# One reciprocal for the softmax sums of two attention units

## What is computed

```python
# nsa_mixer: 16 heads; compressed, selected and windowed keys, each output gated
o = g[..., 0:1] * o_cmp + g[..., 1:2] * o_sel + g[..., 2:3] * o_win
# swa_sink_mixer: 16 heads, window of 128 keys, a sink logit per head
m = jnp.maximum(jnp.max(s, axis=-1, keepdims=True), sk)
e = jnp.exp(s - m)
p = e / (jnp.sum(e, axis=-1, keepdims=True) + jnp.exp(sk - m))
# neighbourhood_attention (8 heads, 512 keys, with a bias) and
# memory_cross_attention (4 heads, 256 keys): p = softmax(s)
```

## Time and profile before

| | |
|---|---|
| median of 3 runs | 2753.83 us (2752.65 to 2754.45) |
| the profiled execution | 2753.48 us, its span 2751.7 us |
| PE busy | 2563.0 us, 93% of the span |
| POOL busy | 1775.8 us, 65% |
| DVE busy | 1378.4 us, 50%, in 2631 instructions |
| ACT busy | 698.0 us, 25% |
| mean granted clock of TensorE | 0.962 |

### The profile page before, as it was taken

How to read it: one execution, slowest core, us unless ns; L and a number is a source line. 1 busy time by engine, 2 the same in 40 slices (tenths; PEclk the granted TensorE clock), 3 DMA queues, 4 the chain that set the end, 5 groups by cost and what they waited for, 6 DMA issues and landing times. The chain is left out here.

```text
span 2751.7 us, 36593 instructions
## 1 busy us (share of the span) xinstructions
PE 2563.0 (93%) x11854; PEld 2052.2 (75%) x11854; DVE 1378.4 (50%) x2631; ACT 698.0 (25%) x1475; POOL 1775.8 (65%) x983
## 2 busy tenths in 40 slices
PE   7798888899999888899999899999999899999998
PEld 6676666688888667688888587777777776787876
DVE  6378888433442477422112466666128534652552
ACT  3302777211001227211101222232006323100001
POOL 5364444577777567587777444445779867687784
PEclk9898999999999989999999999999999999999999
DMA  7573000254652220233333222212333223233332
GB/s 254 153 214 118 1 1 16 61 178 158 213 176 84 62 62 26 86 98 99 92 98 93 84 62 62 62 54 62 94 103 65 72 61 111 84 94 97 92 103 73
DMA packets 420546, 260.13 MB, mean 95 GB/s; under 512 B 62844, under 2 KB 411513, under 8 KB 414017
## 3 DMA queue, kind: packets, MB, share of 16 engines
q1 hardware_dynamic: 390811, 191.28, 24.2%
q10 hardware_dynamic: 29606, 67.22, 7.2%
HBM read 254.25 MB, written 8.10 MB: 95 GB/s over the span
## 5 line engine op out<-in xcount | busy, mean ns | idle before, releaser
L654 POOL TENSOR_TENSOR W<-RAW,zeros 128x1024 fp32r<-128x1024 f32 (+2 forms) x355 | 680.5, 1917 | 698.7 <-PE PA L735 335.2
L661 POOL TENSOR_TENSOR W<-RAW,W 128x1024 fp32r<-128x1024 f32 (+2 forms) x355 | 851.7, 2399 | 48.2 <-PE PA L741 22.0
L734 PE MATMUL PA<-H,W 128*128 128x512 f32 x1272 | 506.4, 398 | 6.4 <-DVEq L2289 2.3
L735 PE MATMUL PA<-H,W 128*128 128x512 f32 x1272 | 495.6, 390 | 0.0
L734 PE MATMUL PA<-A,W 128*128 128x512 f32 x944 | 381.1, 404 | 16.0 <-DVE A L1921 10.8
L735 PE MATMUL PA<-A,W 128*128 128x512 f32 x944 | 378.5, 401 | 0.0
L741 PE MATMUL PA<-H,W 128*128 128x512 f32 x1272 | 316.3, 390 | 0.0
L734 PEld LDWEIGHTS PA<-H,W 128*128 128x128 f32 x1272 | 238.9, 188 | 64.2 <-POOL W L654 6.9
L735 PEld LDWEIGHTS PA<-H,W 128*128 128x128 f32 x1272 | 238.8, 188 | 54.5 <-issue 5.5
L741 PEld LDWEIGHTS PA<-H,W 128*128 128x128 f32 x1272 | 238.9, 188 | 49.3
L741 PE MATMUL PA<-A,W 128*128 128x512 f32 x944 | 249.7, 402 | 0.0
(11 more groups left out here) (362 smaller groups left out, 3919.2 us busy)
## 6 DMA issues: line engine op xcount, KB each, us to landing
AD<-in_ada_w_dram ACTq DMA_DIRECT2D x40, 1024.0 KB, 5.5
RAW<-in_w_in_dram SPq DMA_DIRECT2D x160, 256.0 KB, 3.1
RAW<-in_mlp_w_up_dram SPq DMA_DIRECT2D x128, 256.0 KB, 3.1
RAW<-in_mlp_w_down_dram SPq DMA_DIRECT2D x128, 256.0 KB, 3.0
RAW<-in_w_up_dram SPq DMA_DIRECT2D x88, 256.0 KB, 3.1
RAW<-in_nsa_w_in_dram SPq DMA_DIRECT2D x40, 256.0 KB, 4.1
RAW<-in_w_down_dram SPq DMA_DIRECT2D x16, 384.0 KB, 3.4
RAW<-in_swa_w_in_dram SPq DMA_DIRECT2D x20, 256.0 KB, 3.3
```

Of the source, the lines that this page charges most:

```text
L654: e.tensor_tensor(W[0][:, s, 0:kc], RAW[:, s, 0:kc], zeros[:, 0:1].rearrange("p (a b) -> p a b", b=1).broadcast_to([P, kc, P]), ALU.add).t ...
L661: e.tensor_tensor(W[1][:, s, 0:kc], RAW[:, s, 0:kc], W[0][:, s, 0:kc].bitcast(F32), ALU.subtract).then_inc(w_split, 1)
L734: pe.matmul(PA[s][:, 0:n], W[0][:, s, k], hi, start=(k == 0), stop=False)
L735: mm = pe.matmul(PA[s][:, 0:n], W[0][:, s, k], lo, start=False, stop=False)
```

## The change

The plan gets a list `slot`: a column of the statistics for each unit, which counts single units only and starts anew in each plan. In a plan single units stand in even numbers between `all` units, so b0 and b1 always have columns 2k and 2k+1, and b2 and b3 the next two. On DVE the reciprocal of an even slot is left out; behind the mask that follows the odd one's, one instruction over two columns takes both, and raises `inverted` by 2. The wait for `exped` stands ahead of the branch and is kept in every step.

```diff
@@ class Plan, number
+            single = list(itertools.accumulate(int(not self.groups[G]["all"]) for G, _ in self.units))
+            self.slot = [(n - 1) % 8 for n in single]
@@ POOL, scale_weights
-                nk, v = grp["keys"][b], u % 8
+                nk, v = grp["keys"][b], plan.slot[i]
@@ ACT, attention
-                    nk, sink, v = grp["keys"][b], grp["sink"], u % 8
+                    nk, sink, v = grp["keys"][b], grp["sink"], plan.slot[i]
@@ DVE, attention
-                    nk, mask, v = grp["keys"][b], grp["mask"][b], u % 8
+                    nk, mask, v = grp["keys"][b], grp["mask"][b], plan.slot[i]
...
-                    else:
-                        dve.reciprocal(stat[3][:, u % 8:u % 8 + 1], stat[2][:, u % 8:u % 8 + 1]).then_inc(sem("inverted"), 1)
+                    elif plan.slot[i - 1] % 2:
+                        v = plan.slot[i - 1]
+                        dve.reciprocal(stat[3][:, v - 1:v + 1], stat[2][:, v - 1:v + 1]).then_inc(sem("inverted"), 2)
```

## The result

The kernel after takes **2759.8 us** (median of 20 runs, 2756.8 to 2771.2), the kernel before 2752.2 us in the runs beside it (20 runs, 2745.2 to 2754.5). The ratio is **1.0041** (95% interval 1.0031 to 1.0051): slower by 0.4%, some 11 us. The medians alone are 7.6 us apart; the runs of either kernel scatter over 9 us and more. The profiled execution took 2761.91 us, its span is 2759.8 us, and the mean granted clock is 0.961 where it was 0.962.

A forecast was written before the change was run, and what follows sets the result against it. Bounds: DVE and PE fullest in nsa, no single one in swa, POOL in na, DVE nearly empty in ca. Terms -1.0 - 0.1 + 1.1 + 0.2 = +0.2 us gave 2753.7, as a median 2754.0 us; range 2750.5 to 2758.0.

The forecast's parts named there:

- paid once, not eight times: In na, POOL's wait for the later pair costs +1.1 us (0 to +2.2) in total, not in every head.
- if DVE's times stay: Condition in na: with DVE's timing unmoved, POOL lags 1.1 us and later heads find the pair ready.
- in later heads the bias add then falls on L661 in front, which stretches: In na, POOL's L661 lengthens beside DVE's add by as much as the even unit's multiplication no longer does.
- Are DVE's times unmoved?: In na, yes: DVE's 1.28 us wait is for ACT, not POOL, and scores are ready before DVE asks.
- nsa, -1.0: In nsa, a fifth of the 5.1 us for 64 removed reciprocals is gained: -1.0 us, between 0 and -5.1.
- The cover is PE's distance of five units: In nsa, later multiplications on POOL cost 0, because PE runs five units behind.
- swa, -0.1: In swa, removed reciprocals gain the low end, -0.1 us of a possible 2.6; the delay costs 0.
- ca, +0.2: In ca, the last pair's later multiplication costs +0.2 us, between 0 and +1.2, mostly hidden behind other PE work.
- rival C: In swa, POOL comes too late for PE's transposes: 0.1 to 0.5 us in 16 heads, 2 to 8 us; chance 0.09.
- Rival A: In na, the delay is paid per head through late scores: 8 to 15 us, 2761 to 2769 us; chance 0.06.
- Rival B: In nsa and swa, every removed reciprocal counts at least 0.08 us: 2747.4 us, at the far end 2735; chance 0.05.
- Rival D: In nsa and swa, shifted steps move TensorE's granted clock: 2.5 us either way per stretch, 2751.5 to 2756.5 us; chance 0.12.

The follow-up runs named there:

- c1: Kernel after, but single reciprocals in na and for the two units ahead of nsa's `all` unit: ratio to the kernel before 1.0004 (0.9993 to 1.0015).
- d2: Kernel before, single reciprocals kept, with nsa's 128x4 product done twice in each head, the second waiting for the first: ratio 1.0014 (1.0004 to 1.0024).
- c2: c1 plus, in na, the next head's bias add taken two steps earlier: ratio to the kernel before 0.9995 (0.9984 to 1.0005).
- b1: As a run, not the unit: kernel after with na's value split moved behind the pair's reciprocal; one run, 2766.8 us.
- b2: As a run, not the unit: kernel after with na's next-head bias add moved two steps earlier; one run, 2762.2 us.
- b3: As a run, not the unit: kernel after with both na moves, late value split and early bias add; one run, 2752.0 us.

## Why the prediction was wrong

The forecast was 2754.0 us, the measurement 2759.8, above the range. By its own steps:

1. **na, "paid once, not eight times": the step that failed.** It forecast +1.1 us, and na lost 8.7. The first half held: in the head of the earlier trace rows POOL waits 2.2 us for the pair (2.15 forecast), and b2 and b3 together take 3.11 us, against 3.14 forecast. In the second head even the rest came as forecast: L663 (2082.34) took 3.19 us and POOL did not wait. What failed is "if DVE's times stay" with "in later heads the bias add then falls on L661 in front, which stretches". From the fourth head on L663 did not stretch (2.39 us), in the third hardly (2.52); DVE's split of the values did, from 0.43 to 2.00 us, and pushed the add behind L663. The stretch of 4.24 for 3.14 had been read as something that only POOL suffers. The earlier trace rows The contest has two sides, and the side that gives way decides: when POOL gives way, POOL's lag is absorbed, when DVE does, POOL's next wait is renewed. The question "Are DVE's times unmoved?" was answered from what DVE waits for, not from the durations of its instructions, and the 2.35 us of the add at 2083.57 went unread. The second half of that answer failed too: "the scores behind them are ready before DVE asks", but DVE's mask of b2 waits 0.84 us for them (2115.16). How na's 8.7 us divide between the held split and these late scores is not shown: no run takes away one and leaves all else.
2. **nsa, -1.0.** It was +4.0. That removed reciprocals are mostly swallowed was right (c1: 48 of 64 win nothing that can be told). "The cover is PE's distance of five units" left out the compressed unit, whose product and multiplication follow the late pair in the same step and which PE reaches with little slack: 0.2 us of delay (d2) is enough for 2.8 us more of waits. The 4.0 us itself is one execution's; 1.0 to 5.9 us were seen with the same order.
3. **swa, -0.1, and ca, +0.2.** Measured -0.6 and -0.2 in the profiled executions. Over all of the table swa takes 79.6 to 80.0 us with the pairs and 80.2 to 80.8 without, a gain of 0.2 to 1.2. The stage is shorter, not longer, so rival C's price did not occur.
4. **Rival A** had the right shape and price, 8 to 15 us for a delay in every head, and a chance of 0.06. Its chain is there up to a point: PE's transposes wait for POOL, 10.4 us in na where it was 1.7, and DVE then waits for scores, 12.3 us where it was 6.0. But it does so at the mask of b2, and not "in front of the bias add or the b0 mask", and A has no word of the held split. **Rival B** is excluded: with 88 pairs kept (48 in nsa, 32 in swa, 8 in ca) c1's ratio is 1.0004 (0.9993 to 1.0015), while 0.08 us for each would be 7 us, or 0.26%. **Rival D:** nsa's granted clock went from 0.91 to 0.90, and that is not the loss: in the same stretch (262 to 474 us) c2 has 0.88 and 213.7 us, b1 0.91 and 218.8. na's went from 0.98 (2063 to 2163 us) to 0.95 (2062 to 2170): two more stretches of 3.4 us at the lower level, in which PE can lose 3.4 us at the most. b2 has 0.98 again and still 102.1 us, b3 0.96 and 98.8.

The Trainium skill (GPSIMD Engine Reference, section 8, Key points) states that GpSimd shares its SBUF interfaces with VectorE and contends with DVE instructions that have two SBUF inputs. The traces agree, and give the size: 0.43 becomes 2.00 us beside L663. The rests of the transposed weights, which take one input from PSUM (L1896), took 0.66 to 0.69 us in all 32 units of na, four of them wholly beside L663 (as at 2121.02).

## What to carry to other kernels

Before moving an instruction of POOL or DVE, look at which instructions of the other engine it will newly run beside, and whether DVE's reads two operands from SBUF: price the pair as serial, with the wait on whichever of the two is worse, and look in the trace for rows of that kind that are longer than their fellows. A delay is paid once only if the engine that catches up is not held in its turn by the one it catches up with; follow it through a second round. And batching tiny instructions delays the first of them. Here POOL waited for it: nsa and na lost some 13 us, swa won about 1, and where no pair did harm (c1, c2) the time did not change.

## What the runs showed of the hardware

- In the kernel after, every split of 128x256 (0.43 us by itself) that starts 0.44 to 1.54 us into a full L663 ends 0.28 us behind L663's end: starts at 2094.68, 2108.46, 2122.22, 2134.78, 2148.53. The same holds in b2 (2115.11) and b3 (2107.41, 0.29 us).
- The other side can give way: a bias add that starts 0.44 us into L663 runs at its own length, and L663 takes 3.78 us instead of 2.39 (b1, 2128.00). The split at 2094.68 starts as far into L663 and is held, so the distance between the two starts in the trace doesn't tell who gives way. What does was not tried.
- A tiny DVE instruction is held as well: beside POOL's L696, in 10 of 16 heads, a 128x4 product of 0.17 us takes 0.42 to 0.63 and ends within 0.01 us of the multiplication.
- The stretch from the start to nsa's first mask, which no edit touches, took 255.2 to 262.7 us in the profiled executions. Between the two executions of the kernel before (261.6 and 255.2 us) it is 6.4 of the 7.6 us by which their spans differ, so stages are compared here, not spans.
